# A modulation section summed on VectorE during the output projection, and token copies in another order

## The reference

```
m = silu(cond) @ w_mod + b_mod              # 1024 x 6144; shift, scale, gate, twice
h = rmsnorm(x, g_mix) * (1 + sc1) + sh1
x = x + gt1 * (mixer(h) @ w_out)            # mLSTM heads and attention heads side by side
h = rmsnorm(x, g_ffn) * (1 + sc2) + sh2
x = x + gt2 * moe(h)                        # 16 experts of width 512 in 4 groups
```

## Time and profile before

| | us |
|---|---|
| median of 3 runs | 789.82 (789.20 to 793.39) |
| profiled execution | 789.26 |
| its span | 787.4 |
| PE busy | 762.1 (97%) |
| DVE, ACT, POOL busy | 319.6, 160.2, 58.3 |
| HBM read | 286.31 MB |

### The profile page before, as it was taken

The page is one execution under the profiler, slowest core; times in us unless marked ns, Lnnn a source line. Parts: engine busy times, 40 slices in busy tenths (PEclk is TensorE's granted clock), DMA queues, the critical chain, the costliest instruction groups (busy, mean ns, idle before and its releaser), DMA issues.

```text
span 787.4 us, 11517 instructions
## 1 busy us (share of the span) xinstructions
PE 762.1 (97%) x4975; PEld 409.4 (52%) x4979; DVE 319.6 (41%) x523; ACT 160.2 (20%) x368; POOL 58.3 (7%) x70
## 2 busy tenths in 40 slices
PE   6999999999999999999899999999999999999997
PEld 5655646885434443444245646688643444344424
DVE  1106899625313232123238956772432223213222
ACT  3111224503212011020012111361321211102002
POOL 0410052001100000000010004200110000000000
PEclk9999999999999999999999999999999999999999
DMA  8999599796999999999999980679989999999993
GB/s 311 369 358 410 231 383 411 313 399 241 428 420 424 422 422 424 425 418 424 421 405 394 390 323 1 225 284 380 366 343 402 426 425 420 423 427 419 425 421 149
DMA packets 52980, 289.46 MB, mean 368 GB/s; under 512 B 3448, under 2 KB 5808, under 8 KB 27840
## 3 DMA queue, kind: packets, MB, share of 16 engines
q1 hardware_dynamic: 51200, 285.30, 89.9%
q0 software_dynamic: 1488, 3.31, 1.3%
q10 hardware_dynamic: 240, 0.08, 0.1%
HBM read 286.31 MB, written 2.37 MB: 367 GB/s over the span
## 4 chain that ended last, share of the span: by engine, by line
PE 79%; DMA 11%; DVE 5%; SPq 2%; issue 2%; ACT 1%; DVEq 0%; ACTq 0%
PE ps L1190 23%; PE ps L836 13%; PE ps L1220 12%; PE ps L1107 7%; DMA ring<-in_w_e_up 5%; PE ps L1174 4%; DMA ring<-in_w_e_down 4%; PE ps L854 4%; DMA ring<-in_w_mod 2%; PE ps L1235 2%; PE ps L684 2%; SPq L624 1%; PE ps L698 1%; DVE pT L1803 1%; PE ps L1202 1%
## 5 line engine op out<-in xcount | busy, mean ns | idle before, releaser
L1190 PE MATMUL ps<-ring,xe 128*64 128x512 f32 x688 | 151.6, 594 | 4.3 <-DMA ring<-in_w_e_up 4.3
L836 PE MATMUL ps<-ring,hT 128*128 128x512 f32 (+1 forms) x320 | 125.7, 551 | 0.0
L1190 PEld LDWEIGHTS ps<-ring,xe 128*64 128x64 f32 x688 | 48.6, 137 | 105.3 <-issue 100.3
L1220 PE MATMUL ps<-ring,ex 128*32 128x512 f32 x736 | 92.3, 594 | 0.8 <-DMA ring<-in_w_e_down 0.6
L836 PEld LDWEIGHTS ps<-ring,hT 128*128 128x128 f32 x320 | 60.1, 190 | 60.7 <-issue 58.4
L2123 DVE COPY ye<-ps 64x512 f32<-64x512 f32 (+1 forms) x28 | 19.3, 689 | 164.5 <-PE ps L1220 164.3
L1107 PE MATMUL ps<-hT,ring 128*128 128x256 f32 x256 | 57.1, 381 | 0.0
L2107 DVE RECIPROCAL ex<-ex 128x512 f32<-128x512 f32 x16 | 53.6, 3353 | 0.6
L1220 PEld LDWEIGHTS ps<-ring,ex 128*32 128x32 f32 x736 | 26.0, 110 | 53.0 <-issue 49.4
L1107 PEld LDWEIGHTS ps<-hT,ring 128*128 128x128 f32 x256 | 48.0, 190 | 7.2 <-issue 0.8
L2105 DVE TENSOR_SCALAR ex<-ex 128x512 f32<-128x512 f32 x16 | 6.8, 427 | 110.5 <-ACT ex L1624 110.5
(11 more groups left out here) (281 smaller groups left out, 827.4 us busy)
## 6 DMA issues: line engine op xcount, KB each, us to landing
ring<-in_w_mod SPq DMA_DIRECT2D x24, 2048.0 KB, 16.8
ring<-in_w_e_up SPq DMA_DIRECT2D x23, 2048.0 KB, 19.9
ring<-in_w_e_gate SPq DMA_DIRECT2D x20, 2048.0 KB, 23.1
ring<-in_w_e_down SPq DMA_DIRECT2D x19, 2048.0 KB, 23.1
beside<-in_w_e_gate SPq DMA_DIRECT2D x8, 2048.0 KB, 22.0
ring<-in_w_in SPq DMA_DIRECT2D x7, 2048.0 KB, 20.4
beside<-in_w_e_down SPq DMA_DIRECT2D x7, 2048.0 KB, 20.2
beside<-in_w_e_up SPq DMA_DIRECT2D x5, 2048.0 KB, 18.4
```

Source lines behind the costliest of these rows:

```text
L836: mm = pe.matmul(bank[:, 0:width], hT[:, k, b * P:(b + 1) * P], w[:, k, :], start=(k == 0), stop=(k == KD - 1))
L1190: mm = pe.matmul(bank[PLACES * j:PLACES * j + PLACES, :], xe[:, k, c:c + PLACES], w[:, j, i, :], start=(k == 0), stop=(k == KD - 1))
L1220: mm = pe.matmul(bank[32 * g:32 * g + 32, :], hidT[:, k, c:c + SLOTS], w[j][:, k, half * 512:(half + 1) * 512], start=(k == 0), stop=(k == ...
```

## The change

`FILLER` now has two groups, for layer 0 only, and `LATE` is 1024. VectorE multiplies the first 1024 columns of each of the eight rows k of the last section with the condition and sums them over k (`late_sums`), for context and latent condition apart, into `latesum`; the calls stand between the residuals of the output projection. PE adds the partitions with eight matmuls (`late_rows`). In layer 0 the other 1024 columns are still multiplied on PE (`rows_past_late`, all eight rows); in layer 1 there are none. The block tok 1 moves ahead of "pos", token block 0 is copied by ScalarE and block 1 by VectorE, the section's row is copied behind the blocks, and its columns are transposed behind the gather of the first four experts. SP waits for `late_step` of VectorE, in layer 1 for it alone except at the last slot. `ex` and `hid` become one tile, which holds one of the sums before the experts need it; the other lies in half of `ye`.

```diff
@@ -127,7 +127,8 @@
     return [(l, 1), (l, 2), (l + 1, 0) if l + 1 < DEPTH else (l, 3)]
 
 
-FILLER = (((0,), (1, 2), (3, 4), (5,), (6, 7)), ((0, 1), (2, 3, 4, 5), (6, 7), (), ()))
+FILLER = ((0, 1, 2, 3), (4, 5, 6, 7))
+LATE = KD * P
 BETWEEN = ({"akv": (0, 1), "mo": (2, 3)}, {"mk": (0,), "mq": (1, 2), "mv": (3,)})
 SUM_TURNS = (((0, 1), (2,), (3, 4, 5)), (tuple(range(6)), (6, 7), ()))
 SUM_ROWS = tuple(sum(len(turn) for turn in turns) for turns in SUM_TURNS)
@@ -371,11 +372,14 @@
             over = sb("over", [P, KD * WB], where=experts)
             lists = sb("lists", [P, KD, TOK], where=experts)
             xe = sb("xe", [P, KD, 4 * PLACES], where=experts)
-            ex = sb("ex", [P, F], where=experts)
-            hid = sb("hid", [P, KF, P], where=experts)
+            exhid = sb("exhid", [P, 2 * F], where=experts)
             ye = sb("ye", [P, NB, D], where=experts)
             rt = sb("rt", [P, 11, 32], where=experts)
             beside = sb("beside", [P, len(BESIDE), KD * WB], where=experts)
+        ex = exhid[:, 0:F]
+        hid = exhid[:, F:2 * F].rearrange("p (k q) -> p k q", k=KF)
+        latesum = (exhid[:, :], ye[:, 1, :])
+        latelone = rt[:, 0:2, :].rearrange("p i n -> p (i n)")
         sq2 = xe
         h2 = lists
         htok = hT.ap().rearrange("p k t -> p (k t)").rearrange("p (b k c) -> p b k c", b=NB, k=KD)
...
@@ -531,8 +535,13 @@
 
                 if key[0] == "mod":
                     _, ml, ms, i = key
+                    if (ml, ms) in (last_section(0), last_section(1)):
+                        done_rows = KD // section_slots(ml, ms) * (i + 1)
+                        sp.wait_ge(late_step, NB * (KD * (ms == 3) + done_rows))
                     if ms == 1 and i < section_slots(ml, ms) - 1:
                         sp.wait_ge(sum_step, sum_steps(ml) + 2 * NB * (i + 1))
+                    elif ms == 3 and i < section_slots(ml, ms) - 1:
+                        pass
                     elif i < section_slots(ml, ms) - 1:
                         sp.wait_ge(mod_read, section_reads(ml, ms, i + 1))
                     else:
@@ -670,6 +679,33 @@
                 for i in which:
                     rows_of_section(l, s, *range(rows_in_slot * i, rows_in_slot * (i + 1)))
 
+            def late_rows(l, s):
+
+                bank = begin(("modrow", l, s))
+                pe.wait_ge(late_step, NB * KD * (l + (s == 3)))
+                for b in range(NB):
+                    for g in range(4):
+                        mm = pe.matmul(bank[32 * g:32 * g + 32, 0:LATE // 4], latelone[:, 31 - b:63 - b],
+                                       latesum[b][:, g * LATE // 4:(g + 1) * LATE // 4], start=(b == 0), stop=(b == NB - 1))
+                if s == 3:
+                    done(("modrow", l, s), mm)
+
+            def rows_past_late(l, s, *ks):
+
+                n = section_slots(l, s)
+                width, rows_in_slot = LATE // 4, KD // n
+                bank = ps[banks["modrow", l, s][0]]
+                for k in ks:
+                    i, row = k // rows_in_slot, k % rows_in_slot
+                    w = landed(("mod", l, s, i)).rearrange("p (k n) -> p k n", k=rows_in_slot)
+                    for g in range(4):
+                        mm = pe.matmul(bank[32 * g:32 * g + 32, width:2 * width], cT[:, NB * k:NB * k + 32],
+                                       w[:, row, LATE + g * width:LATE + (g + 1) * width], start=(k == 0), stop=(k == KD - 1))
+                    if k == KD - 1:
+                        done(("modrow", l, s), mm)
+                    elif row == rows_in_slot - 1:
+                        mm.then_inc(mod_read, 1)
+
             def rows_of_section(l, s, *ks):
 
                 n = section_slots(l, s)
@@ -1123,13 +1159,14 @@
                 for b in range(NB):
                     pe.matmul(bank[:, b * E:(b + 1) * E], ident[0:NB, b:b + 1].broadcast_to([NB, P]), sdot[:, :],
                               start=False, stop=False, skip_group_check=True)
-                rows_of_section(*fill, *FILLER[l][0])
+                late_rows(*fill)
                 for b in range(NB):
                     taken(pe, (("logits", b), l))
                     mm = pe.matmul(bank[:, b * E:(b + 1) * E], lr[:, b * P:(b + 1) * P], cst[:, C_SELR:C_SELR + E],
                                    start=False, stop=(b == NB - 1), skip_group_check=True)
                 done(("router", l), mm)
-                rows_of_section(*fill, *FILLER[l][1])
+                if l + 1 < DEPTH:
+                    rows_past_late(*fill, *FILLER[0])
 
                 def token_rows(i):
 
@@ -1146,7 +1183,9 @@
                     done((("tok", i), l), mm)
 
                 token_rows(0)
-                rows_of_section(*fill, *FILLER[l][2])
+                if l + 1 < DEPTH:
+                    rows_past_late(*fill, *FILLER[1])
+                token_rows(1)
 
                 bank = begin(("pos", l))
                 pe.wait_ge(mask_ready, l + 1)
@@ -1154,15 +1193,11 @@
                 pe.matmul(bank[:, 0:E], keep[:, 0, :], m[0], start=True, stop=True)
                 done(("pos", l), pe.matmul(bank[:, E:2 * E], keep[:, 0, :], m[1], start=True, stop=True))
                 token_rows(2)
-                rows_of_section(*fill, *FILLER[l][3])
                 bank = begin(("count", l))
                 for b in range(NB):
                     mm = pe.matmul(bank[:, b * E:(b + 1) * E], ones[:, :], m[b], start=True, stop=True)
                 done(("count", l), mm)
-                rows_of_section(*fill, *FILLER[l][4])
-                token_rows(1)
                 token_rows(3)
-                section_columns(*fill)
 
                 def gather(q, *which):
 
@@ -1300,6 +1335,7 @@
                 pe.wait_ge(pick_ready, 2 * l + 1)
                 taken(pe, *[(("tok", i), l) for i in range(4)])
                 gather(0, 0, 1, 2, 3)
+                section_columns(*fill)
                 for p in range(PAIRS):
                     pair(p)
 
@@ -1600,15 +1636,19 @@
                 modulate(l, 1, sq2, 0, range(1, 4))
                 act.wait_ge(xr_ready, XR_STEPS * l + 5)
                 modulate(l, 1, sq2, 0, range(4, KD))
-                act.wait_ge(xr_ready, XR_STEPS * l + 7)
-                modulate(l, 1, sq2, 1, (6, 7))
-                for i in (2, 1, 3):
-                    if i == 1:
-                        section_row(*last_section(l))
+                def token_copy(i):
+
                     key = (("tok", i), l)
                     bank = full(act, key)
                     act.activation(htok[:, i // 2, :, 64 * (i % 2):64 * (i % 2) + 64],
                                    bank[:, :].rearrange("p (k q) -> p k q", k=KD), ACT.Copy).then_inc(free(key), 1)
+
+                token_copy(0)
+                act.wait_ge(xr_ready, XR_STEPS * l + 7)
+                modulate(l, 1, sq2, 1, (6, 7))
+                token_copy(2)
+                token_copy(3)
+                section_row(*last_section(l))
 
                 def pick_out(q, *which):
                     for i in which:
@@ -1692,11 +1732,14 @@
                 key = ("modcol", l, s)
                 bank = full(dve, key)
                 first, chunks = SECTION_CHUNKS[l, s]
-                span, n = slice(first, first + chunks), section_slots(l, s)
-                dve.tensor_tensor(modc[:, l % 2, span, :].rearrange("p (g j) b -> p g j b", g=4),
-                                  bank[:, 0:n * P].rearrange("p (j g r) -> p g j r", j=n, g=4)[:, :, :, 0:NB],
-                                  per_col(cols[:, l, span].rearrange("p (g j) -> p g j", g=4), NB),
-                                  ALU.add).then_inc(free(key), 1)
+                parts = 2 if (l, s) == last_section(0) else 1
+                n = section_slots(l, s) // parts
+                for part in range(parts):
+                    span = slice(first + part * chunks // parts, first + (part + 1) * chunks // parts)
+                    ins = dve.tensor_tensor(modc[:, l % 2, span, :].rearrange("p (g j) b -> p g j b", g=4),
+                                            bank[:, part * n * P:(part + 1) * n * P].rearrange("p (j g r) -> p g j r", j=n, g=4)[:, :, :, 0:NB],
+                                            per_col(cols[:, l, span].rearrange("p (g j) -> p g j", g=4), NB), ALU.add)
+                ins.then_inc(free(key), 1)
                 taken(dve, key)
                 if s in (0, 2):
                     which, scale, g = (0, KD, A_GMIX) if s == 0 else (1, 4 * KD, A_GFFN)
@@ -2006,6 +2049,26 @@
                     ins = dve.tensor_scalar(cat[:, MH + h, P:2 * P], bank[:, h * P:(h + 1) * P],
                                             cols[:, l, A_GMH + h:A_GMH + h + 1], None, ALU.mult)
                 ins.then_inc(free(key), 1)
+                def late_sums(*ks):
+
+                    ml, ms = last_section(l)
+                    rows_in_slot = KD // section_slots(ml, ms)
+                    for k in ks:
```

(26 more changed lines are left out.)

2 lines of the change are left out of this document (1 added, 1 removed).

## The result

The changed kernel takes 793.05 us in the median of 20 runs (792.08 to 795.14); the kernel before, on the same chip, 789.74 us (788.45 to 793.39, 20 runs). The ratio is 1.0044, with a 95% interval of 1.0037 to 1.0052: the change costs 3.3 us. The profiled execution of the changed kernel took 793.07 us, span 791.2.

A forecast was written before the change was run, and what follows sets the result against it. The continuous stream of expert loads was taken as the bound, not PE. Layer 0 0.0, VectorE 0.0 and layer 1 +0.55 on the profiled 789.26 gave 789.8; with the median 0.56 above, 790.4 us, range 787.1 to 793.0.

The forecast's parts named there:

- Layer 0, gain 0.0: Layer 0's expert stage: PE gains 2.6 us, which become wait for `w_e_up` in pair 7; 0.0 us on the path.
- VectorE, cost 0: Both layers: VectorE's added sums, 1.19 us apart, fit its idle time, residual 3 staying at 183.74 us; cost 0.
- The late columns, +0.55 us: Layer 1: columns behind the gather delay a load from 572.8 to 577.3 us, so the stream's tail is 0.55 us later.
- The gather of layer 1 "starts at 573.1": Layer 1's router: gather starts at 573.1 instead of 573.45 us, pair 0 at 577.1, within 0.1 of before.
- this case as a rival: Clock falls in layer 1's router without filler, low for 2 to 4 us, losing 1 to 3; 792.4 at 2 us; chance 0.25.
- that PE is the bound: Rival: 2.6 us of layer 0 and 0.1 of layer 1 are kept, median 787.1 us; chance 0.12.
- that VectorE overruns: Rival: sums spaced beyond 1.28 us delay residual 3 in both layers; 795.6 us at 1.5 us spacing; chance 0.08.
- that nothing moves: Rival: late sums in layer 1's ring or a bank wait undo the change, streams as before, 789.8 us; chance 0.07.

The follow-up runs named there:

- `l0only`: The change made in layer 0 only, layer 1's filler, loads and token blocks as in the kernel before; 790.40 us, 1.0004 of the kernel before.
- `before_latecols`: The kernel before with one edit: layer 1's section columns transposed behind the gather instead of ahead of it; 790.30 us, 1.0008 of the kernel before.
- `warm1`: The changed kernel plus empty 512-column matmuls in layer 1's router, 9 in the first wait and 3 in the second; 790.23 us.
- `l1only`: The change in layer 1 only against the kernel before, but layer 0's modulation-column bias added in two parts, so values differ; 792.99 us, 1.0047.
- `l1only_b`: The change in layer 1 only against the kernel before, layer 0's modulation-column bias added in one piece as before; 793.17 us, 1.0048.
- `cols1`: The changed kernel with layer 1's section row and columns put back ahead of the gather; 791.41 us, 1.002 of the kernel before.
- `before_thin`: The kernel before with each of layer 1's 32 filler matmuls narrowed from 256 to 16 columns; 791.72 us, 1.0026 of the kernel before.
- `warm_second`: The changed kernel plus 3 empty matmuls in the second wait of layer 1's router, none in the first; 791.78 us, 1.0026 of the kernel before.

## Why the prediction was wrong, step by step

- **Layer 0, gain 0.0: right.** The gather was put near 197 us and pair 0 near 201.2; with the 0.54 us of the head they stand at 196.8 and 201.0. The saved PE time turned into waits for `w_e_up`, the last block did not move, and `l0only` is within 0.15% of the kernel before.
- **VectorE, cost 0: right.** 1.19 us was the spacing taken between the ends of 1.13 and 2.26, and it is what the trace shows.
- **The late columns, +0.55 us: right in the mechanism**, by the closed hole in `before_latecols`. Its interval, [0.9999, 1.0016], holds 0.55 us and just reaches zero. The prediction set beside it the Trainium skill's fit of 2.0 us and 436 GB/s (DMA: Bandwidth & Descriptors, Anatomy of one DMA), which that section gives for transfers issued by GpSimd, while SyncE issues the loads here; the sum went by the trace's rate, and the changed kernel shows 423 GB/s again.
- **The gather of layer 1 "starts at 573.1" and lasts 3.81 us: this is the step that failed.** The starts were worked out with the durations of the earlier trace rows, which were measured at 2.4 GHz, although filler that PE had run there was gone. With the head's 0.54 us taken off, the gather was due at 572.6; it started at 574.37, 1.8 us late, as the small pieces ran at half clock, and it took 2.4 us more. The sum, 4.2 us, is what pair 0 lost (580.72 where 576.5 was due). In `warm1`, with the clock held, gather and pair 0 come where they were predicted. The load behind the columns is late by the same, and, the stream having no slack from there on, so is the end. Between the two profiled executions the account closes: counted from layer 1's output projection pair 0 is 4.1 us late and the end 4.4, that projection comes 0.6 us earlier, and 3.8 us is what lies between 793.07 and 789.26. Put on the forecast instead, 790.4 + 4.2 - 0.5 gives 794.1, 1 us above the measured 793.05: the forecast holds 0.56 us between median and profiled execution, which the changed kernel does not show, and the 0.55 us of the columns do not come on top in full once pair 0 is late.
- The prediction had this case as a rival and gave it a quarter. It weighed two grounds: that the earlier trace rows shows the clock at 0.50 after a stretch of light work, and that "elsewhere waits of 2 to 3 us left the clock at 2.4 GHz". The second was the weak one. It read waits, not load: the new stretch holds a wait of 2.38 us, no longer than those, but with 0.64 us of work in 3.90 around it. The price was off as well: 2 to 4 us at the low level were assumed, and it was 10.2, so that its 792.4 was still too low.
- What the changed kernel and `warm_first` differ in is 9 matmuls that nothing reads, and they are 793.05 and 789.41 us (ratios 1.0044 and 1.0001). By the rule of the Trainium skill (TensorE: Matmul & The Clock Gate, What's actually happening) that the throttled state is the default and activity releases it, such work is worth something without a result; the trace agrees.
- The other rivals: that PE is the bound is refuted by the last up block of layer 0, that VectorE overruns by residual 3, and that nothing moves by the first pair.

## What to carry to other kernels

Matmuls that fill a wait on TensorE may pay for themselves by the clock they hold, not only by what they compute; before moving them to another engine, add up what is left in each stretch that they filled, and price the case in which everything up to the next dense block runs at half clock. A dense block behind such a stretch pays too: the gather ran its first 5.0 us at the low level. And where a stage is bound by a stream of loads, the number that matters is the issue at which the stream becomes continuous; what TensorE saves behind that is only returned as waiting.

## What the runs showed of the hardware that was not expected

- In layer 1's router the low level lasted 10.2 us in the profiles of the changed kernel, `l1only`, `l1only_b`, `cols1` and `before_thin`, though PE shows as busy for most of it (8.81 of 9.70 us in the changed kernel); in `warm_second` it lasted 3.4. Why it was shorter there stays open.
- When it began differed between executions with the same matmuls up to there: 38.6, 37.5, 38.3 and 36.9 us behind the start of layer 1's output projection in the changed kernel, `l1only`, `l1only_b` and `cols1`. The gather's price differed with it, 2.4, 1.9, 2.2 and 1.6 us.
- At 0.50 of the clock a transposing group of four takes 1.09 us instead of 0.63, and the gather, which returned to full clock in its last 1.2 us, 6.21 us instead of 3.81.
- With 9 empty matmuls of 512 columns, 2.13 us, in the first wait the clock stayed at 2.4 GHz up to the gather; with 3 in the second wait alone it fell, at 569.0 us, as without any.
